# Gate and up projections of a SwiGLU feed-forward as Strassen products, with the on-chip memory laid out anew

## The chip, the cores and the metric

The kernel runs on one core of a Trainium2 chip. What is measured is the time of one execution on the device in microseconds (us), from the first to the last instruction and what lies around them. Smaller is better. The core has five engines that work beside each other and wait for each other through semaphores: TensorE (PE, matmul), VectorE (DVE), ScalarE (ACT), GpSimd (POOL) and SyncE (SP, which here only issues DMAs). Matmul results go to PSUM, eight banks of 128 x 512 floats; everything else lies in SBUF.

## The reference

Two decoder layers over 1024 tokens of width 1024 in float32. Each layer mixes tokens in three head groups, maps them by one output projection, and then runs the dense feed-forward on which the change works (D_FF = 2816):

```python
mix = jnp.concatenate([hm, ha, hs], axis=-1) @ w_out
x = x + rms_norm(mix, norm_w[1])
h = rms_norm(x, norm_w[2])
ff = (jax.nn.silu(h @ w_gate) * (h @ w_up)) @ w_down
return x + rms_norm(ff, norm_w[3])
```

`h @ w_gate` and `h @ w_up` are each 1024 x 1024 by 1024 x 2816; `@ w_down` is 1024 x 2816 by 2816 x 1024.

## The kernel before

Every engine runs one fixed instruction list, written out by hand; waits on counted semaphores (`d_hi(L, n)` is "n of layer L are done") tie the lists together. Nothing is reordered. A layer has three stages. Stage A makes the input projection, the indexer and the attention; stage B scans the chunks of the two recurrent groups and then runs the output projection and its norms; stage E is the feed-forward, and its last part is interleaved with the norm at the start of the next layer.

**Splitting.** A float32 product is made of three fp32r matmuls: each operand is split into a rounded part (`hi`, a copy on ACT) and the rest (`lo`, a subtraction), and hi\*hi + hi\*lo + lo\*hi is accumulated. A weight tile costs one ACT copy and one POOL subtraction.

**Output projection (end of stage B).** For each of the eight token tiles t (128 tokens) PE runs 48 matmuls of 128 x 512 into two PSUM banks. Then ACT takes the mean square (`stats`, count `d_s1`), DVE scales (`mixn`, `d_mix`) and adds the residual (`xres`, `d_x`), ACT takes the mean square again (`d_s2`), DVE scales (`mixn` again, `d_xn`), PE transposes the tile (`turn_normed`, 8 small matmuls, `d_turn`), ACT copies it out of PSUM as `act_hi` (`hi(t)`, `d_hi`) and DVE subtracts to get `act_lo` (`lo(t)`, `d_lo`). PE works on tile t+1 meanwhile.

**Feed-forward (stage E).** FB = 11 blocks of 256 hidden columns. A block has four units (gate and up for each of two groups of 128 columns). A unit is the product of a 1024 x 128 weight tile with all 1024 tokens: two halves of 512 tokens, 8 slices of the inner dimension, 3 matmuls each, so 48 matmuls of 128 x 512 (`half_unit`, L2125). ACT applies SiLU to the gate unit from PSUM (`gate`), DVE multiplies with the up unit from PSUM into `hf` (`hid`, L2189), ACT and POOL split `hf` into `hhi` and `hlo`. `down` then runs 96 matmuls (L2157), 12 for each token tile, and DVE adds each tile's two banks into `yacc` (L2196). PE does gate and up of block b, then down of block b-1; the last down follows on the down of the block before it. Each weight tile is a 512 KB DMA into one of two `raw` buffers, split by ACT (L2048) and POOL (L2002). At the entry PE begins with the first halves of gate and up for tokens 0 to 511 while tile 7 is still being normalised:

```python
half_unit(0, 0)
turn_normed(pe, NT - 1)
pe.wait_ge(*w_lo(L, U_FF + 2))
pe.wait_ge(*d_mix(L, NT))
half_unit(1, 0)
pe.wait_ge(*d_lo(L, NT))
half_unit(0, 1)
half_unit(1, 1)
```

**End of the layer.** Per token tile, behind its part of the last down: `yacc` add on DVE, mean square on ACT, scaling on DVE (L2219), residual add on POOL (L2041, which waits for all eight `resid` loads), and in layer 0 a mean square, a scaling (L402), a transposition on PE (L2145) and a split for layer 1.

SBUF is allotted by stacks that overlay the stages.

## Time and profile before

| | |
|---|---|
| median of 3 runs | 2903.09 us (2901.5 to 7317.59) |
| the profiled execution | 2905.06 us, of which the span is 2903.3 us |
| PE busy | 97% of the span, 13396 matmuls |
| DVE, ACT, POOL busy | 42%, 32%, 31% |
| mean granted TensorE clock | 0.984 |

The profiled execution is 2 us above the median; the sum of the prediction is made against it. A busy share counts time in which an engine has an instruction under way. Matmuls overlap in the pipeline (one takes 389 ns from start to end, yet the next starts earlier), so what a matmul costs is read from the spacing of starts.

### The profile page before, as it was taken

How to read it: one execution, taken by the hardware profiler on the slowest of the kernel's cores; microseconds unless marked ns; L12 is line 12 of the kernel's file. 1: busy time of each engine (PE TensorE's matmuls, PEld its weight loads, DVE VectorE, ACT ScalarE, POOL GpSimd, SP SyncE). 2: the span in 40 equal slices, each digit the busy share in tenths (PEclk: the TensorE clock that was granted, in tenths of full speed). 3: DMA queues.
4: the chain of work that ended last, by engine and by line, in shares of the span. 5: the costliest groups of instructions: out<-in, count | busy, mean ns of one | idle time of the engine just before them, and what ended most of it. 6: DMA issues, size and time to landing. Idle time of an engine off the chain costs nothing. (4 is left out here: it accounts for less than half of the span.)

```text
span 2903.3 us, 34251 instructions
## 1 busy us (share of the span) xinstructions
PE 2810.1 (97%) x13396; PEld 2261.9 (78%) x13396; DVE 1229.7 (42%) x2170; ACT 924.5 (32%) x1618; POOL 906.3 (31%) x450
## 2 busy tenths in 40 slices
PE   6999999999999999999989999998999999999997
PEld 5677877778888888888766788777788888888886
DVE  4479854574111122211355799547640122211115
ACT  4336433563211111111243374346632111111112
POOL 1238410330332333222343383104303232222234
PEclk9999999899999999999999999999999999999999
DMA  4102310522211111111321133106221111111113
GB/s 131 44 23 87 116 57 19 151 88 95 74 44 51 58 43 58 43 43 43 116 80 30 30 95 111 59 15 179 81 89 50 58 44 57 43 43 43 51 45 137
DMA packets 232832, 197.72 MB, mean 68 GB/s; under 512 B 20352, under 2 KB 208896, under 8 KB 232592
## 3 DMA queue, kind: packets, MB, share of 16 engines
q1 hardware_dynamic: 226960, 175.26, 20.0%
q10 hardware_dynamic: 5760, 20.97, 1.9%
q8 instruction: 70, 1.15, 0.2%
q14 instruction: 42, 0.34, 0.0%
HBM read 157.41 MB, written 38.80 MB: 68 GB/s over the span
## 5 line engine op out<-in xcount | busy, mean ns | idle before, releaser
L2125 PE MATMUL ps<-act_hi,whi 128*128 128x512 f32 x1408 | 548.4, 389 | 0.0
L2125 PE MATMUL ps<-act_hi,wlo 128*128 128x512 f32 x1408 | 548.1, 389 | 0.0
L2125 PE MATMUL ps<-act_lo,whi 128*128 128x512 f32 x1408 | 547.7, 389 | 0.0
L2189 DVE TENSOR_TENSOR hf<-sg,ps 128x1024 f32<-128x1024 f32 x44 | 53.7, 1221 | 891.4 <-PE ps L2125 891.4
L834 PE MATMUL ps<-act_hi,whi 128*128 128x512 f32 x960 | 395.2, 412 | 15.5 <-ACT smr L383 10.6
L834 PE MATMUL ps<-act_hi,wlo 128*128 128x512 f32 x960 | 378.9, 395 | 0.0
L834 PE MATMUL ps<-act_lo,whi 128*128 128x512 f32 x960 | 378.6, 394 | 0.0
L2002 POOL TENSOR_TENSOR wlo<-raw,whi 128x1024 fp32r<-128x1024 f32 x88 | 210.0, 2395 | 489.3 <-ACT whi L2048 489.3
L1247 DVE TENSOR_SCALAR_CACHE_REDUCE ties<-score,kth 128x384 uint8<-128x384 f32 (+5 forms) x396 | 348.4, 943 | 5.1 <-issue 0.4
L2196 DVE TENSOR_TENSOR yacc<-yacc,ps 128x1024 f32<-128x1024 f32 x176 | 214.8, 1220 | 248.5 <-PE ps L2157 248.5
L2125 PEld LDWEIGHTS ps<-act_lo,whi 128*128 128x128 f32 x1408 | 264.3, 188 | 55.2
L2125 PEld LDWEIGHTS ps<-act_hi,wlo 128*128 128x128 f32 x1408 | 264.3, 188 | 55.1
L2125 PEld LDWEIGHTS ps<-act_hi,whi 128*128 128x128 f32 x1408 | 264.3, 188 | 54.6
L2054 ACT ACTIVATE sg<-ps 128x1024 f32<-128x1024 f32 x44 | 45.2, 1028 | 712.8 <-PE ps L2125 712.8
L536 POOL TENSOR_TENSOR wlo<-raw,whi 128x1024 fp32r<-128x1024 f32 x56 | 137.0, 2447 | 405.4 <-ACT whi L578 405.4
L834 PEld LDWEIGHTS ps<-act_hi,whi 128*128 128x128 f32 x960 | 182.8, 190 | 90.6 <-issue 49.0
L2157 PE MATMUL ps<-dlo,hhi 128*128 128x512 f32 x640 | 249.2, 389 | 0.0
L2157 PE MATMUL ps<-dhi,hhi 128*128 128x512 f32 x640 | 249.1, 389 | 0.0
L2157 PE MATMUL ps<-dhi,hlo 128*128 128x512 f32 x640 | 249.1, 389 | 0.0
L834 PEld LDWEIGHTS ps<-act_hi,wlo 128*128 128x128 f32 x960 | 182.8, 190 | 40.0
L834 PEld LDWEIGHTS ps<-act_lo,whi 128*128 128x128 f32 x960 | 183.3, 191 | 36.1 <-issue 1.9
L2007 POOL TENSOR_TENSOR hlo<-hf,hhi 128x1024 fp32r<-128x1024 f32 x44 | 105.8, 2405 | 330.5 <-ACT hhi L2058 330.5
(304 smaller groups left out, 3974.6 us busy)
## 6 DMA issues: line engine op xcount, KB each, us to landing
raw<-in_w_in SPq DMA_DIRECT2D x56, 512.0 KB, 3.9
raw<-in_w_up SPq DMA_DIRECT2D x44, 512.0 KB, 4.0
raw<-in_w_gate SPq DMA_DIRECT2D x44, 512.0 KB, 3.8
raw<-in_w_down SPq DMA_DIRECT2D x44, 512.0 KB, 3.6
proj_scratch<-stage ACTq DMA_DIRECT2D x40, 512.0 KB, 2.7
wc<-proj_scratch SPq DMA_DIRECT2D x14, 1280.0 KB, 6.7
xmid_scratch<-xres SPq DMA_DIRECT2D x16, 512.0 KB, 2.6
resid<-xmid_scratch SPq DMA_DIRECT2D x14, 512.0 KB, 5.5
```

The source lines that it names most:

```text
L536: pool.tensor_tensor(wlo[u % 2][:, :], raw[u % 2][:, :], whi[u % 2][:, :].bitcast(F32), ALU.subtract)\
L834: mm = pe.matmul(ps[:, half, :], w[:, k], a[:, k, cols], start=(k == 0 and m == 0), stop=(k == KT - 1 and m == 2))
L1247: v.tensor_scalar(tie(c), of(c), at(kth, c), 0.0, op, ALU.add, accum_out=at(held, c))
L2002: pool.tensor_tensor(lo_t[s][:, :], raw[s][:, :], hi_t[s][:, :].bitcast(F32), ALU.subtract)\
L2007: pool.tensor_tensor(hlo[p][:, j], hf[:, :], hhi[p][:, j].bitcast(F32), ALU.subtract).then_inc(h_lo.sem, 1)
L2054: act.activation(sg[:, :], unit_psum(0), ACT.Silu).then_inc(silu.sem, 1)
L2125: mm = pe.matmul(ps[:, 2 * s + half, :], w[:, k], a[:, k, cols], start=(k == 0 and m == 0), stop=(k == KT - 1 and m == 2))
L2157: mm = pe.matmul(place(t)[:, cols], h[p][:, j, rows], w[j][:, cols], start=(j == 0 and m == 0), stop=(j == 1 and m == 2))
L2189: v.tensor_tensor(hf[:, :], sg[:, :], unit_psum(1), ALU.mult).then_inc(hidden.sem, 1)
L2196: v.tensor_tensor(yacc[:, t], yacc[:, t], place(t), ALU.add).then_inc(y_add.sem, 1)
```

## The change

**Strassen.** The gate product of a pair of units (256 hidden columns) is seen as a 2 x 2 by 2 x 2 product: the weights in four quadrants (half of the inner dimension by unit), the tokens in four (half of the inner dimension by 512 tokens). Instead of eight quadrant products, 96 matmuls, PE makes seven, of 12 matmuls each (`product`). The same is done for up. The seven token operands ("token forms": five sums of quadrants and two plain quadrants) are made once a layer and kept in SBUF, split in hi and lo. The seven weight operands ("weight forms") are made for every product: DVE adds two quadrants (five of seven), ACT copies the hi part, POOL subtracts the lo part, in a ring of six slots of 128 x 512. A slot is taken again when PE has finished with it (`f_done`).

**Results.** A product lands in one PSUM bank (banks 0 to 3 in turn; down uses 4 to 7). ACT writes the first product to two quarters of the result in SBUF, DVE adds or copies the other six into their quarters, 10 operations of 128 x 512. SiLU and the multiplication by up then run on quarters in SBUF (4 each per block instead of 2 of 128 x 1024 from PSUM).

**Order.** PE's turn k: seven products of up (k), seven of gate (k+1), then down (k), 96 matmuls as before. Gate 0 is the entry; after the tenth turn come up (10) and down (10), one behind the other. The weights come as 1 MB loads of 256 columns.

**Entry.** The token forms need float32 quadrants: ACT copies each transposed tile to `normed_q` (`untransposed`, two operations), the token sums run on DVE, their hi copies on ACT, their lo parts on DVE and POOL. They and the first weight forms are put between the steps of tiles 5, 6 and 7. The forms of tokens 0 to 511 in tiles 4 to 6 come first (`EARLIER`), tile 7 later (`LAST`). `yacc` lies where the quadrants were, so POOL clears it only when the last token form is done.

**Memory.** SBUF is placed by address. The constant table (1.3 MB) is overlaid by `yacc` and loaded again in layer 1; the small weights of layer 1 and the norm rows are loaded near the end of stage E instead of at its start. The identity for transpositions has a place of its own, so that `cst` in matmuls becomes `ident`.

The core of the diff:

```diff
+        WEIGHT_SUM = {1: ((0, 1), (1, 1), ALU.subtract), 2: ((0, 0), (1, 1), ALU.add), 3: ((1, 0), (0, 0), ALU.subtract),
+                      4: ((1, 0), (1, 1), ALU.add), 6: ((0, 0), (0, 1), ALU.add)}
+        WEIGHT_PART = {0: (1, 1), 5: (0, 0)}
+        TOKEN_SUM = {0: ((0, 0), (0, 1), ALU.add), 2: ((0, 0), (1, 1), ALU.add), 4: ((0, 1), (1, 1), ALU.subtract),
+                     5: ((1, 0), (1, 1), ALU.add), 6: ((1, 0), (0, 0), ALU.subtract)}
+        TOKEN_PART = {1: (0, 0), 3: (1, 1)}
+        SUMMED = {1: 1, 2: 2, 3: 3, 4: 4, 6: 5}
+        PRODUCT_BANK = (0, 1, 2, 3, 0, 1, 2)
...
+            def token_sum(v, i, cols):
+
+                (a, b, op), d = TOKEN_SUM[i], form_sum[i]
+                v.tensor_tensor(d[:, :, cols], normed_q[a[0]][a[1]][:, :, cols], normed_q[b[0]][b[1]][:, :, cols], op)\
+                 .then_inc(t_sum.sem, 1)
...
+            def first_form_hi(act, i):
+
+                if i in WEIGHT_SUM:
+                    act.wait_ge(*f_sum(L, SUMMED[i]))
+                    src = flat_form(ring_sum[(i + 5) % 6])
+                else:
+                    act.wait_ge(*f_in[0](L, 16))
+                    src = weight_part(ff_raw[0], *WEIGHT_PART[i])
+                act.activation(flat_form(ring_hi[(i + 5) % 6]), src, ACT.Copy).then_inc(f_hi.sem, 1)
...
-                for s in range(2):
-                    pool.wait_ge(*w_hi(L, U_FF + s + 1))
-                    if s == 1:
-                        pool.wait_ge(*wo_lo_v(L, KT - WO_POOL))
-                    pool.tensor_tensor(wlo[s][:, :], raw[s][:, :], whi[s][:, :].bitcast(F32), ALU.subtract).then_inc(w_lo.sem, 1)
+                pool.wait_ge(*t_hi(L, 1))
+                token_lo(pool, 1, EVERY, t_lo_p)
+                first_form_lo(pool, 0)
+                pool.wait_ge(*t_hi(L, 2))
+                token_lo(pool, 0, EVERY, t_lo_p)
+                for i in range(1, 4):
+                    first_form_lo(pool, i)
 
...
+                def untransposed(t):
                     act.wait_ge(*d_turn(L, t + 1))
-                    act.activation(act_hi[:, :, t * P:(t + 1) * P], tiles(turn_bank(t)), ACT.Copy).then_inc(d_hi.sem, 1)
+                    for j in range(2):
+                        ins = act.activation(normed_q[t // 4][j][:, :, (t % 4) * P:(t % 4 + 1) * P], tiles(turn_bank(t))[:, 4 * j:4 * j + 4],
+                                             ACT.Copy)
+                    ins.then_inc(d_hi.sem, 1)
...
+                    if t == NT - 1:
+                        act.wait_ge(*t_sum(L, 2))
+                        token_hi(act, 2, EARLIER)
...
+                    if t == 5:
+                        act.wait_ge(*d_hi(L, 4))
+                        token_hi(act, 1, EVERY)
+                        first_form_hi(act, 0)
+                    if t == 6:
+                        act.wait_ge(*t_sum(L, 1))
+                        token_hi(act, 0, EVERY)
+                        for i in range(1, 4):
+                            first_form_hi(act, i)
+                token_hi(act, 3, EARLIER)
+                act.wait_ge(*t_sum(L, 3))
+                token_hi(act, 4, EARLIER)
+                untransposed(NT - 1)
+                act.wait_ge(*t_sum(L, 4))
+                token_hi(act, 2, LAST)
+                act.wait_ge(*d_hi(L, NT))
+                token_hi(act, 3, LAST)
+                act.wait_ge(*t_sum(L, 5))
+                token_hi(act, 4, LAST)
+                first_form_hi(act, 4)
+                first_form_hi(act, 5)
+                for i in (5, 6):
+                    act.wait_ge(*t_sum(L, i + 1))
+                    token_hi(act, i, EVERY)
...
                 for t in range(NT):
                     s = t % 2
-                    if t == 2:
-                        lo(0)
+                    if t == NT - 1:
+                        v.wait_ge(*d_mm(L, NT))
+                        v.wait_ge(*d_hi(L, NT - 1))
+                        token_sum(v, 2, EARLIER)
...
+                    if t == NT - 1:
+                        token_sum(v, 4, EARLIER)
...
+                    if t == 6:
+                        for i in range(1, 4):
+                            first_sum(v, i)
+
+                def lo(i, cols, at_hi):
+                    v.wait_ge(*t_hi(L, at_hi))
+                    token_lo(v, i, cols, t_lo_v)
+
+                lo(2, EARLIER, 3)
+                v.wait_ge(*d_xn(L, NT))
+                first_sum(v, 4)
+                lo(4, EARLIER, 5)
+                v.wait_ge(*d_hi(L, NT))
+                token_sum(v, 2, LAST)
+                token_sum(v, 4, LAST)
+                lo(2, LAST, 6)
+                lo(3, LAST, 7)
+                lo(4, LAST, 8)
+                token_sum(v, 5, EVERY)
+                token_sum(v, 6, EVERY)
+                lo(5, EVERY, 9)
...
+                pool.wait_ge(*t_hi(L, 4))
+                token_lo(pool, 3, EARLIER, t_lo_p)
                 if N < DEPTH:
-                    clear_small(pool)
-                for i in range(2):
-                    pool.memset(yacc[:, 4 * i:4 * i + 4], 0.0).then_inc(y_add.sem, 1)
-                for b in range(3):
-                    body(b, b % 2, U_FF + max(6 * b - 2, 0))
+                    clear_columns(pool)
+                first_form_lo(pool, 4)
+                first_form_lo(pool, 5)
+                form_lo_part(6, 6, 5, (0, 1))
+                pool.wait_ge(*t_lo_v(L, 7))
+                pool.wait_ge(*t_lo_p(L, 3))
+                for t in range(NT):
+                    ins = pool.memset(yacc[t][:, :], 0.0)
+                    if t % 4 == 3:
+                        ins.then_inc(y_add.sem, 1)
...
+                k, f0 = FB - 1, cycle(FB - 1)
+                form_lo_part(6, f0 + 6, 0, (1, 0))
+                for q in range(4):
+                    down_lo(q, f0 + 7 + q, 1 + q, (0, 0))
+                    if q == 1:
+                        hid_lo(k, 0)
+                if N < DEPTH:
+                    pool.wait_ge(*f_lo(L, N_FORMS))
+                    clear_small(pool)
+                for n in range(1, 4):
+                    hid_lo(k, n)
...
+                def first_product(t, f):
+
+                    act.wait_ge(*f_done(L, f + 1))
+                    act.activation(quarter_of(t, 0, 1), ps[:, PRODUCT_BANK[0], :], ACT.Copy)
+                    act.activation(quarter_of(t, 0, 0), ps[:, PRODUCT_BANK[0], :], ACT.Copy, scale=-1.0).then_inc(m_first.sem, 1)
...
+                def product(i, f, slot, r):
+
+                    pe.wait_ge(*f_lo(L, f + 1))
+                    later = not (isinstance(r, int) and r == 0)
+                    if i == 0 and later:
+                        pe.wait_ge(*m_drain(L, 10 * (r - 1) + DRAINED[4]))
+                    if i == 1 and later:
+                        pe.wait_ge(*m_drain(L, 10 * (r - 1) + DRAINED[5]))
+                    if i == 2 and later:
+                        pe.wait_ge(*m_drain(L, 10 * (r - 1) + DRAINED[6]))
+                    if i == 4:
+                        pe.wait_ge(*m_first(L, r + 1))
+                    if i == 5:
+                        pe.wait_ge(*m_drain(L, 10 * r + DRAINED[1]))
+                    if i == 6:
+                        pe.wait_ge(*m_drain(L, 10 * r + DRAINED[2]))
+                    wh, wl = flat_form(ring_hi[slot]), flat_form(ring_lo[slot])
+                    for k in range(4):
+                        for m, (w, a) in enumerate(((wh, form_hi[i]), (wh, form_lo[i]), (wl, form_hi[i]))):
+                            mm = pe.matmul(ps[:, PRODUCT_BANK[i], :], w[:, k], a[:, k], start=(k == 0 and m == 0), stop=(k == 3 and m == 2))
+                    mm.then_inc(f_done.sem, 1)
+
...
+                def turn_of(k):
+                    f0 = cycle(k)
+                    for i in range(7):
+                        product(i, f0 + i, i % 6, up_item(k))
+                    for i in range(7):
+                        product(i, f0 + 7 + i, (i + 1) % 6, gate_item(k))
+                    down(k, f0 + 14, (2, 3, 4, 5), turn_bank)
+
...
+                product(0, 0, 5, 0)
+                product(1, 1, 0, 0)
                 turn_normed(pe, NT - 1)
-                pe.wait_ge(*w_lo(L, U_FF + 2))
                 pe.wait_ge(*d_mix(L, NT))
-                half_unit(1, 0)
-                pe.wait_ge(*d_lo(L, NT))
-                half_unit(0, 1)
-                half_unit(1, 1)
-                gate_up(0, U_FF)
...
+                def drain(t, i, f, r):
+
+                    def add(quarter, op, after):
+                        q = quarter_of(t, *quarter)
+                        v.wait_ge(*m_drain(L, 10 * r + after))
+                        v.tensor_tensor(q, q, ps[:, PRODUCT_BANK[i], :], op).then_inc(m_drain.sem, 1)
+
+                    def copy(quarter):
+                        v.tensor_copy(quarter_of(t, *quarter), ps[:, PRODUCT_BANK[i], :]).then_inc(m_drain.sem, 1)
+
+                    v.wait_ge(*f_done(L, f + 1))
+                    if i == 1:
+                        v.wait_ge(*m_first(L, r + 1))
+                        q = quarter_of(t, 0, 1)
+                        v.tensor_tensor(q, q, ps[:, PRODUCT_BANK[i], :], ALU.add).then_inc(m_drain.sem, 1)
+                        copy((1, 1))
+                    if i == 2:
+                        q = quarter_of(t, 0, 0)
+                        v.tensor_tensor(q, q, ps[:, PRODUCT_BANK[i], :], ALU.add).then_inc(m_drain.sem, 1)
```

**ScalarE, from the second mean square of tile 6 to the last tile, layer 0.** `normed10` and `normed11` are float32 quadrants, `form_hi2` the hi part of token form 2, `ring_hi0` that of a weight form in slot 0. Before:

```order
L1392 ACTIVATE mixn0,small<-xres0 128x1024 [waits d_x]
L1394 ACTIVATE small<-small 128x1 [waits d_s2]
L1396 ACTIVATE small<-small 128x1 [waits d_s2]
L1392 ACTIVATE mixn1,small<-ps 128x1024 [waits d_turn,d_mm]
L1394 ACTIVATE small<-small 128x1 [waits d_s1]
L1396 ACTIVATE small<-small 128x1 [waits d_s1]
L1787 ACTIVATE act_hi<-ps 128x8x128 [waits d_turn]
L1392 ACTIVATE mixn1,small<-xres1 128x1024 [waits d_x]
```

Now:

```order
L1458 ACTIVATE form_hi0<-form_sum0 128x2048 [waits t_sum]
L1483 ACTIVATE ring_hi0<-ring_sum0 128x512 [waits f_sum]
L1483 ACTIVATE ring_hi1<-ring_sum1 128x512 [waits f_sum]
L1483 ACTIVATE ring_hi2<-ring_sum2 128x512 [waits f_sum]
L1506 ACTIVATE mixn1,small<-ps 128x1024 [waits d_turn,d_mm]
L1508 ACTIVATE small<-small 128x1 [waits d_s1]
L1510 ACTIVATE small<-small 128x1 [waits d_s1]
L1903 ACTIVATE normed10<-ps 128x4x128 [waits d_turn]
L1903 ACTIVATE normed11<-ps 128x4x128
L1458 ACTIVATE form_hi2<-form_sum2 128x4x384 [waits t_sum]
L1506 ACTIVATE mixn1,small<-xres1 128x1024 [waits d_x]
```

Four copies stand between the last mean square of tile 6 and the first of tile 7, three of which wait for sums of DVE.

**VectorE, the same place, from the last scaling of tile 6 on.** `ring_sum` is a float32 weight sum, `form_sum` a token sum. Before:

```order
L1929 SCALAR_TENSOR_TENSOR mixn0<-xres0,small,nrow1 128x1024 [waits d_s2]
L1921 SCALAR_TENSOR_TENSOR mixn1<-ps,small,nrow0 128x1024 [waits d_s1]
L1925 TENSOR_TENSOR xres1<-xres1,mixn1 128x1024 [waits xr_in1,d_mix]
L1913 TENSOR_TENSOR act_lo<-ps,act_hi 128x8x128 [waits d_hi]
L1929 SCALAR_TENSOR_TENSOR mixn1<-xres1,small,nrow1 128x1024 [waits d_s2]
```

Now:

```order
L1472 TENSOR_TENSOR ring_sum0<-ff_raw0 128x512 [waits f_in0]
L1472 TENSOR_TENSOR ring_sum1<-ff_raw0 128x512
L1472 TENSOR_TENSOR ring_sum2<-ff_raw0 128x512
L1449 TENSOR_TENSOR form_sum2<-normed00,normed11 128x4x384 [waits d_hi,d_mm]
L2054 SCALAR_TENSOR_TENSOR mixn1<-ps,small,nrow0 128x1024 [waits d_s1]
L2058 TENSOR_TENSOR xres1<-xres1,mixn1 128x1024 [waits xr_in1,d_mix]
L1449 TENSOR_TENSOR form_sum4<-normed01,normed11 128x4x384
L2062 SCALAR_TENSOR_TENSOR mixn1<-xres1,small,nrow1 128x1024 [waits d_s2]
L1462 TENSOR_TENSOR form_lo2<-form_sum2,form_hi2 128x4x384 [waits t_hi]
L1472 TENSOR_TENSOR ring_sum3<-ff_raw0 128x512 [waits d_xn]
L1462 TENSOR_TENSOR form_lo4<-form_sum4,form_hi4 128x4x384 [waits t_hi]
```

Two token sums stand among the steps of tile 7, and two lo parts and a sum behind them.

**GpSimd at the entry of the feed-forward.** `ring_lo0` is the lo part of a weight form. Before:

```order
L357 MEMSET smw 128x1024
L358 MEMSET bcol 128x4
L2029 MEMSET yacc 128x4096 x2
L2002 TENSOR_TENSOR wlo0<-raw0,whi0 128x1024
L2007 TENSOR_TENSOR hlo0<-hf,hhi0 128x1024
```

Now:

```order
L1462 TENSOR_TENSOR form_lo3<-normed11,form_hi3 128x4x384
L415 MEMSET bcol 128x4
L1489 TENSOR_TENSOR ring_lo3<-ring_sum3,ring_hi3 128x512
L1489 TENSOR_TENSOR ring_lo4<-ff_raw0,ring_hi4 128x512
L2177 TENSOR_TENSOR ring_lo5<-ring_sum5,ring_hi5 128x512
L2219 MEMSET yacc0 128x1024
...
L2219 MEMSET yacc7 128x1024
L2177 TENSOR_TENSOR ring_lo0<-ff_raw1,ring_hi0 128x512
L2177 TENSOR_TENSOR ring_lo1<-ring_sum1,ring_hi1 128x512
```

The clearing has moved from before the first split of the stage to between the forms of gate 0 and those of up 0.

## Rows read from the trace of the kernel before

**Rows 1.** The page, busy time (share of the span) and instructions of each engine.

```profile
PE 2810.1 (97%) x13396; PEld 2261.9 (78%) x13396; DVE 1229.7 (42%) x2170; ACT 924.5 (32%) x1618; POOL 906.3 (31%) x450
```

**Rows 2.** The chain that ended last, layer 1: start us, us, what.

```profile
2173.74 81.62 PE ps L2125 x360
2255.36 21.79 PE ps L2157 x96
2277.16 43.55 PE ps L2125 x192
```

**Rows 3.** Busy time of each engine from 740 to 1400 us (feed-forward, layer 0).

```profile
740.00:1400.00 660.00, 660.00 (x2911) 546.17 (x2910) 114.79 (x94) 104.12 (x106) 199.66 (x84) 1.00 0.18 51
```

**Rows 4.** Timeline of DVE and ACT, operations of 128 x 512: start, us, engine, line.

```profile
628.63 0.68 DVE L1880 TENSOR_TENSOR smem<-smem,ps 128x512 f32<-128x512 f32 x1
628.22 0.60 ACT L1732 ACTIVATE act_hi<-ps 128x512 fp32r<-128x512 f32 x1 [1.12 <-PE ps L1565]
```

**Rows 5.** Operations of 128 x 1024 by line: ns min/median/max; and ACT's copy.

```profile
L2196 DVE TENSOR_TENSOR yacc<-yacc,ps x176: 1205/1221/1224, 823.4 to 2891.0; 128x1024 f32<-128x1024 f32 x176
L2002 POOL TENSOR_TENSOR wlo<-raw,whi x88: 2382/2396/2407, 751.9 to 2850.7; 128x1024 fp32r<-128x1024 f32 x88
750.79 1.05 ACT L2048 ACTIVATE whi<-raw 128x1024 fp32r<-128x1024 f32 x1
```

**Rows 6.** Timeline of POOL and of DVE at the start of layer 1.

```profile
1468.61 3.46 POOL L374 TENSOR_TENSOR wlo<-smw,whi 128x1024 fp32r<-128x1024 f32 x1
1472.04 3.35 POOL L2041 TENSOR_TENSOR resid<-resid,yacc 128x1024 f32<-128x1024 f32 x1
1468.59 1.27 DVE L2219 SCALAR_TENSOR_TENSOR yacc<-yacc,small,nrow 128x1024 f32<-128x1024 f32 x1
1470.33 2.83 DVE L402 SCALAR_TENSOR_TENSOR yacc<-hf,small,nrow 128x1024 f32<-128x1024 f32 x1 [0.47 <-ACT small L391]
```

**Rows 7.** Timeline of PE around tile 7, layer 0.

```profile
731.22 0.48 PE L2125 MATMUL ps<-act_hi,whi 128*128 128x512 f32 x1
...
737.81 1.09 PE L1387 MATMUL ps<-cst,mixn 128*128 128x128 f32 x8 [0.88 <-DVE mixn L1929]
738.66 0.47 PE L2125 MATMUL ps<-act_hi,whi 128*128 128x512 f32 x1
```

**Rows 8.** Timeline of ACT and DVE around tiles 6 and 7, layer 0.

```profile
722.75 1.06 ACT L1392 ACTIVATE mixn<-xres 128x1024 f32<-128x1024 f32 x1 [1.69 <-DVE xres L1925]
...
730.62 1.03 ACT L1392 ACTIVATE mixn<-ps 128x1024 f32<-128x1024 f32 x1 [6.26 <-PE ps L1635]
...
724.40 1.28 DVE L1929 SCALAR_TENSOR_TENSOR mixn<-xres,small,nrow 128x1024 f32<-128x1024 f32 x1 [0.55 <-ACT small L1396]
732.24 1.28 DVE L1921 SCALAR_TENSOR_TENSOR mixn<-ps,small,nrow 128x1024 f32<-128x1024 f32 x1 [6.56 <-ACT small L1396]
733.56 1.23 DVE L1925 TENSOR_TENSOR xres<-xres,mixn 128x1024 f32<-128x1024 f32 x1
```

**Rows 9.** Timeline of POOL at the entry of the feed-forward, layer 0.

```profile
739.89 6.98 POOL L2029 MEMSET yacc<- 128x4096 f32 x2
```

**Rows 10.** Timeline of PE at the start of layer 1: spacing of matmuls behind a wait.

```profile
1472.22 0.47 PE L834 MATMUL ps<-act_hi,whi 128*128 128x512 f32 x1 [4.04 <-POOL wlo L374]
...
1474.26 0.63 PE L834 MATMUL ps<-act_hi,whi 128*128 128x512 f32 x1
1474.68 0.63 PE L834 MATMUL ps<-act_lo,whi 128*128 128x512 f32 x1
```

**Rows 11.** Timeline of PE at the first matmul of the last down, layer 0.

```profile
1430.30 0.40 PE L2157 MATMUL ps<-whi,hhi 128*128 128x512 f32 x1
```

**Rows 12.** The tail of layer 1 on POOL, DMA around the residual loads of layer 0 (window), and DMA issues (KB, us to landing).

```profile
2873.41 2.41 POOL L2041 TENSOR_TENSOR resid<-resid,yacc 128x1024 f32<-128x1024 f32 x1 [20.36 <-DVE yacc L2219]
1410.00:1420.00 10.00, 10.00 (x46) 1.00 0.57 218
cst<-in_table SPq DMA_DIRECT2D x1, 1344.5 KB, 7.3
```

More of the change, by code:

```diff
@@ L160, in build, with at @@
         minus_b = sb("minus_b", [P, P], BF16)
-        mix_mem = ExitStack()
-        def mb(name, shape, dt=F32):
-            return sb(name, shape, dt, mix_mem)
+        def at(place, name, shape, dt=F32):
+            gap = ExitStack()
+            if place:
+                sb("to_" + name, [P, place // 4], F32, gap)
+            t = sb(name, shape, dt, gap)
+            gap.close()
+            return t
+        KB = 1024
+        act_hi = [at(32 * KB * h, f"act_hi{h}", [P, KT, HALF], F32R) for h in range(2)]
@@ L252, in build, with after @@
[L252 to L257 removed]
+        top = [MIX]
+        def after(name, shape, dt=F32):
+            t = at(top[0], name, shape, dt)
+            n = (4 if dt != U8 else 1) * int(np.prod(shape[1:]))
+            top[0] += -(-n // 32) * 32
+            return t
@@ new lines, in build @@
+        avr = after("avr", [P, NT, AH * HD])
+        aq = after("aq", [P, 2, S])
+        ak = after("ak", [P, 2, S])
+        iq = after("iq", [P, 2, S])
+        stage = [after(f"stage{s}", [P, 3 + S]) for s in range(2)]
+        ik = after("ik", [P, S])
+        smr = after("smr", [P, S])
+        ties = after("ties", [P, sum(width[2:])], U8)
+        kth = after("kth", [P, NT - 2])
+        held = after("held", [P, NT - 2])
+        TAIL = CHUNKS + 101536
+        DOWN0 = TAIL - 4 * KB
+        assert top[0] <= TAIL - 12 * KB
@@ L2139, in turn_next, with down @@
+                def down(k, f, slots, place, turning=False):
                     def turn_next(t):
```

788 lines of the change are left out of this document (462 added, 326 removed).

## The prediction

> **What bounds the kernel now.** I read the page first. PE is busy for 97% of the span, the other engines for 31 to 42% [rows 1]. A busy share alone does not name the bound, so the chain of work that ended last comes next: from 2173.74 us on it is PE alone through the whole feed-forward, in a pattern that repeats every 65.34 us, 192 gate and up matmuls in 43.55 us and 96 down matmuls in 21.79 us [rows 2]. Both give 0.227 us for a matmul of 128 x 512. The third view is the busy time by window: over 660 us of the feed-forward PE is busy without a break at a granted clock of 1.00, while DVE works 115 us, ACT 104 and POOL 200 [rows 3]. So in this stage the number of matmuls is the time, and the others have room. Around the stage, where tiles are normalised, chains through ACT, DVE and POOL decide, and PE has little slack.
>
> **Fewer matmuls.** A product pair has 7 x 12 = 84 matmuls instead of 96. A layer has 11 blocks with two such pairs, so 22 x 12 = 264 matmuls fall away, 528 in all. At 0.227 us [rows 2] that is 119.8 us, all on the path.
>
> **The work added per block (hidden).** A block becomes 168 + 96 = 264 matmuls, 59.9 us. Prices for 128 x 512: DVE 0.68 us, ACT 0.60 [rows 4]; POOL half of 2.40 = 1.20 [rows 5]. DVE: 20 result operations, 10 weight sums and 4 multiplications are 34 x 0.68 = 23, and 8 `yacc` adds of 1.22 [rows 5] make 33 us. ACT: 4 first results, 18 weight copies, 4 SiLU, 4 hidden copies, 30 x 0.60 = 18 us. POOL: 18 weight and 4 hidden subtractions, 22 x 1.20 = 26 us. All stay under 59.9.
>
> DVE and POOL also block each other. An operation of DVE with both inputs in SBUF took 2.83 us instead of 1.28 while POOL worked: it started at 1470.33 and ended at 1473.16, right after POOL's had ended at 1472.07, and POOL's next, already due, took 3.35 us instead of 2.40, so the one that waits gets the port between two instructions of the other [rows 6]. An operation with one input in PSUM never waits (1205 to 1224 ns in 176 cases beside POOL's work) [rows 5]. The weight sums and the four multiplications are of the first kind. If all 14 waited for a whole POOL operation, DVE would be held 33 + 17 = 50 us, still under 59.9. The Trainium skill, "SBUF — State Buffer", section "Who interferes with whom", states the same as a lock: a DVE instruction with two SBUF inputs and a GpSimd instruction that reads SBUF exclude each other for a whole instruction. It speaks against the change, since the sums are all of that kind; without it the entry below would come to 14.6 us a layer instead of 24.3, and the time to 2829 instead of 2849 us. The trace agrees with the rule.
>
> The tightest place of the ring is behind down (k). Two products are ready (5.44 us of PE), the third needs DVE's last `yacc` add, its sum, ACT's copy and POOL's subtraction: 1.22 + 0.68 + 0.60 + 1.20 = 3.7 us, or 5.5 with one wait for the other engine's operation at each of the two (1.20 and 0.60). It fits; I take 0. The loads: the 1.3 MB table lands in 7.3 us [rows 12]; a 1 MB weight load is let go when the forms of the previous product are made, which is at least 8 us before its first use. I take 0.
>
> **The entry to the feed-forward (twice).** Times from 730.62, when ACT begins with tile 7 in layer 0 [rows 8]. Before: PE starts the first 24 matmuls at +0.6, waits 0.88, transposes tile 7 at +7.2 and never stops from +8.0 on [rows 7]. Now, with prices scaled by length (DVE 128 x 1536 1.7, x 2048 2.25; ACT 1.5 and 1.95; POOL 3.6 and 4.8 us, from rows 4 and 5):
> - Tile 6 runs up to 0.3 late behind POOL's work; DVE ends its last scaling at -4.7 (before: 724.40 + 1.28 = -4.9) [rows 8]. The three weight sums follow, but POOL's 4.8 us subtraction for token form 0 starts at about -3.5 among them, until +1.3. The third sum ends at +2.0, ACT's copy of it at +2.6.
> - ACT's mean square of tile 7 stands behind that copy: 2.5 instead of 0. Until 4.0; then the two copies of tile 6 to 5.1. DVE's token sum 2 needs those and waits for POOL's three weight parts: 5.6 to 7.3. Then scaling 8.5, residual 9.8, mean square 11.4, scaling behind token sum 4 12.8. PE transposes tile 7 at +12.9 instead of +7.2. It has made its two products by +6.8.
> - ACT first copies forms 3 and 4 (to 14.4), then tile 7 (15.5). DVE's lo of form 2 runs to 14.4, POOL's of form 3 to 18.0, and DVE's next sum waits for it; sum, lo of form 4, two sums for tile 7 and the lo of form 2 end at 22.4. Product 2 starts at +22.4, where PE before had done as many matmuls at +8.0: **14.4 us lost**.
> - From there product 4 needs bank 0 free; ACT copies that only behind token forms 5 and 6, at +11.3. Product 5 needs DVE's two results of product 1, at +14.5, behind two sums and two lo parts of 2048 and two waits for POOL. The last lo part ends at +12.6, the lo of weight form 6 at +15.1; then POOL clears `yacc` in 7.1 us (6.98 before for the same size) [rows 9] and makes the first form of up 0: +23.5. Five products take 13.6 us: **9.9 lost**.
>
> Together 24.3 us a layer. Pauses also cost clock: after a pause of 4.04 us the spacing went to 0.43 us [rows 10] for some 7 matmuls, 1.2 GHz in place of 2.4, about 1.5 us; I take one such per entry. So 2 x 25.8 = 51.6 us. Bounds: without any mutual blocking the same queues give tile 7 transposed at +9.7, product 2 at +15.5 and up 0 20.7 after it, 7.5 + 7.1 = 14.6 lost, 2 x 14.6 = 29; at the other end 2 x 29 = 58 with one more POOL operation waited for at each half and a second spell of half clock.
>
> **The end of the feed-forward (twice).** Before, the last down follows the one before it without a gap, its first matmul 0.23 us after the last of that [rows 11], because its hidden units were made meanwhile. Now it follows up (10). Behind the last product stand: DVE result and multiplication, ACT copy, POOL subtraction, 0.68 + 0.68 + 0.60 + 1.20, and POOL still has the third quarter's subtraction in front. Worked through the queues it is 3.6 us, and 4.4 in layer 0, where the clearing of `smw` stands there too. With 1 us of half clock each: 10.0 us in all (6 to 14).
>
> **The change of layers and the rest.** The `resid` loads start only in the last block. Eight of 512 KB and two norm rows at 218 GB/s [rows 12], 2.4 us each, land about 26 us after product 2 of up (10), some 3 us after POOL could use them in layer 0; in layer 1 the tail begins 8.1 us after its last down starts, at 2873.41 [rows 12], and the loads are just in time. I take 2 us (0 to 5). The reloaded table is asked for only about 15 us later: 0. Stages A and B keep their instructions: 0.
>
> **Sum.** 2905.06 - 119.8 + 51.6 + 10.0 + 2.0 = 2848.9 us, 1.9% under the median of 2903.09. (The profiled execution is 2 us above it, which I leave in.) The bounds give 2820 to 2862. About 2% is what a measurement of this kernel can tell from no change; that line is 2845.
>
> **Rivals.**
> 1. *The entry is cheaper.* The chains above add up waits between three queues, each decided by tenths of a microsecond; with no mutual blocking they give 2829. For it: a POOL operation that comes just later finds DVE between two waits. Against: the rows show the block every time the two meet. 2829, chance 0.18.
> 2. *Something recurs in every turn.* The third form behind down has 5.44 us for 3.7 to 5.5. If it comes 1 us late, 20 turns of 1 us give 2869. For it: three engines hand over in a row. Against: all have room. Chance 0.16.
> 3. *Slower than before.* The same place, but with a pause long enough to drop the clock: 4 us and 1.5 us of half rate, as in rows 10, in each of 20 turns are 110 us, 2959. It is slower than before from 2.8 us a turn on (56 us over 20), so if that form takes over 8 us. Nothing in rows 4 to 6 reaches that. Chance 0.05.
> 4. *The saving is not taken by PE.* If what 12 matmuls save is waited for elsewhere, for PSUM banks or sums, the time would be 2905 + 64 - 120 x (share saved); with half saved 2909. Against: each bank is free 4 products before it is needed again. Chance 0.05.
>
> The forecast itself has 0.56, spread over 2835 to 2862. The range 2826 to 2873 leaves out rivals 3 and 4 and the edges of 1 and 2.
>
> **Chances.** Faster by over 2% (under 2845): rival 1 and about 0.24 of the forecast's 0.56, 0.43 with some hundredths for gains not seen. Slower by over 2% (over 2961): 0.03. Within 2%: 0.54.
>
> **What would show it.** In the feed-forward 264 matmuls of 0.227 us per block and no wait of PE longer than some tenths inside the turns. At the entry a first mean square of tile 7 that starts about 2.5 us after its matmuls, a transposition near +12.9, product 2 near +22, waits of PE for DVE's lo part, for ACT's first result and for POOL's first form behind the memsets. At the end a pause of about 4 us before the last down. I am wrong if PE waits in each turn, if DVE's adds from PSUM are slowed by POOL, or if the chains of tile 7 are much shorter than queued here.

## The result, and the profile after

The changed kernel takes 2873.56 us (median of 4 runs, 2871.85 to 2875.19) where the kernel before takes 2903.09 (median of 2901.5, 2903.09 and 2908.02; a fourth execution, of 7317.59 us, is left out as slow): a ratio of 0.9896, with a 95% interval of 0.9884 to 0.9909. The change brought some 30 us, not the 56 us that the prediction gave it, and the time lies just above the upper end of the range. Its profiled execution took 2874.07 us, with a span of 2872.2.

The page of the changed kernel, answering to [rows 1]: PE is less busy, DVE and POOL more.

```profile
PE 2737.7 (95%) x12868; PEld 2172.7 (76%) x12868; DVE 1812.2 (63%) x2886; ACT 1117.7 (39%) x2094; POOL 1233.6 (43%) x776
```

The chain of work in layer 1, answering to [rows 2] (start us, us, what):

```profile
2186.13 7.16 POOL yacc L2219 x8
2193.30 1.24 POOL ring_lo L2177
2194.54 0.04 issue
2194.59 39.37 PE ps L2394 x168
2233.95 22.21 PE ps L2419 x96
2256.16 39.12 PE ps L2394 x168
2295.29 22.21 PE ps L2419 x96
```

Read it twice. First, the pattern is what was forecast: 168 and 96 matmuls, PE alone, no pause between the pieces. Second, divide. 39.12 / 168 is 232.9 ns and 22.21 / 96 is 231.4 ns, where before 43.55 / 192 was 226.8 and 21.79 / 96 was 227.0 [rows 2]. Every matmul has the same shape as before and takes about 5.5 ns longer in the mean. A turn is 61.33 us instead of the 59.9 that 264 matmuls of 0.227 make, and from the first matmul of up 0 to the last before the pause at the end 2724 matmuls take 632.9 us instead of 617.8: 15.1 us a layer, 30.2 in all.

It is not the clock, and it is not a busy engine. Busy times from 780 to 1400 us, with the columns of [rows 3]: granted clock 1.00, DVE busy 61% of the time, POOL 53%.

```profile
780.00:1400.00 620.00, 620.00 (x2671) 500.79 (x2670) 375.34 (x427) 176.10 (x304) 330.27 (x225) 1.00 0.17 53
```

The entry of layer 0, on DVE, POOL, ACT and PE, answering to [rows 7] and [rows 8] (start us, us, engine, line):

```profile
724.10 6.30 DVE L1472 TENSOR_TENSOR ring_sum<-ff_raw 128x512 f32<-128x512 f32 x3
...
742.69 3.91 DVE L1472 TENSOR_TENSOR ring_sum<-ff_raw 128x512 f32<-128x512 f32 x1
...
724.76 5.09 POOL L1462 TENSOR_TENSOR form_lo<-form_sum,form_hi 128x2048 fp32r<-128x2048 f32 x1 [4.70 <-ACT form_hi L1458]
...
741.24 4.81 POOL L1462 TENSOR_TENSOR form_lo<-normed,form_hi 128x1536 fp32r<-128x1536 f32 x1 [7.18 <-ACT form_hi L1458]
...
765.01 7.22 POOL L2219 MEMSET yacc<- 128x1024 f32 x8
...
730.97 1.01 ACT L1506 ACTIVATE mixn<-ps 128x1024 f32<-128x1024 f32 x1
...
741.16 1.97 PE L1501 MATMUL ps<-ident,mixn 128*128 128x128 f32 x8 [5.41 <-DVE mixn L2062]
750.36 0.77 PE L2394 MATMUL ps<-form_hi,ring_hi 128*128 128x512 f32 x1 [7.23 <-issue]
...
761.11 0.48 PE L2394 MATMUL ps<-form_hi,ring_hi 128*128 128x512 f32 x1 [2.95 <-ACT gate_t L2270]
```

Three weight sums of 0.68 us took 6.30 us because POOL's subtraction of 5.09 us lay among them, and the one at 742.69 took 3.91 for the same reason. Tile 7's statistics wait for them. Count from the end of the output projection (728.67 + 0.4 = 729.07), which answers to the 730.62 of the prediction: statistics at +1.9, transposition at +12.1, product 2 at +21.3, then product 4 10.8 later and up 0 23.2 later.

The end of the feed-forward, answering to [rows 11]: PE is idle for 4.15 us before the last down, waiting for POOL. From here on a pause is counted from the start of the last matmul before it to the start of the first behind it, here 4.54 us.

```profile
1406.24 0.40 PE L2394 MATMUL ps<-form_hi,ring_lo 128*128 128x512 f32 x1
1410.79 0.76 PE L2419 MATMUL ps<-ring_hi,hhi 128*128 128x512 f32 x1 [4.15 <-POOL hlo L2188]
```

### The profile page after: what moved, and what is told of

Its sections match the earlier page's. It is cut to its first block and busy times, and to the rows that moved or that the text cites. A ratio compares the mean times of both kernels' runs of the same rounds, so it can differ in the third digit from the quotient of the medians.

```text
span 2872.2 us, 36030 instructions
## 1 busy us (share of the span) xinstructions
PE 2737.7 (95%) x12868; PEld 2172.7 (76%) x12868; DVE 1812.2 (63%) x2886; ACT 1117.7 (39%) x2094; POOL 1233.6 (43%) x776
## 5 line engine op out<-in xcount | busy, mean ns | idle before, releaser
L2177 POOL TENSOR_TENSOR ring_lo<-ring_sum,ring_hi 128x512 fp32r<-128x512 f32 x212 | 321.3, 1530 | 508.9 <-ACT ring_hi L2258 508.9
L2394 PE MATMUL ps<-form_hi,ring_hi 128*128 128x512 f32 x1232 | 491.1, 399 | 24.1 <-issue 14.5
L2394 PE MATMUL ps<-form_hi,ring_lo 128*128 128x512 f32 x1232 | 488.9, 397 | 0.0
L2394 PE MATMUL ps<-form_lo,ring_hi 128*128 128x512 f32 x1232 | 488.3, 396 | 0.0
L900 PE MATMUL ps<-act_hi,whi 128*128 128x512 f32 x960 | 396.0, 412 | 14.6 <-ACT smr L440 10.5
L900 PE MATMUL ps<-act_hi,wlo 128*128 128x512 f32 x960 | 380.0, 396 | 0.0
L900 PE MATMUL ps<-act_lo,whi 128*128 128x512 f32 x960 | 379.5, 395 | 0.0
L2419 PE MATMUL ps<-ring_hi,hhi 128*128 128x512 f32 x704 | 281.2, 399 | 8.5 <-POOL hlo L2188 8.1
L2419 PE MATMUL ps<-ring_hi,hlo 128*128 128x512 f32 x704 | 279.6, 397 | 0.0
L2419 PE MATMUL ps<-ring_lo,hhi 128*128 128x512 f32 x704 | 279.3, 397 | 0.0
L2394 PEld LDWEIGHTS ps<-form_hi,ring_lo 128*128 128x128 f32 x1232 | 232.9, 189 | 57.1
L2394 PEld LDWEIGHTS ps<-form_lo,ring_hi 128*128 128x128 f32 x1232 | 233.3, 189 | 56.0
```

Source lines behind the costliest of these rows:

```text
L900: mm = pe.matmul(ps[:, half, :], w[:, k], a[half][:, k, :], start=(k == 0 and m == 0), stop=(k == KT - 1 and m == 2))
L2177: pool.tensor_tensor(flat_form(ring_lo[slot]), src, flat_form(ring_hi[slot]).bitcast(F32), ALU.subtract)\
L2394: mm = pe.matmul(ps[:, PRODUCT_BANK[i], :], w[:, k], a[:, k], start=(k == 0 and m == 0), stop=(k == 3 and m == 2))
L2419: mm = pe.matmul(place(t)[:, cols], h[:, j, rows], w, start=(j == 0 and m == 0), stop=(j == 1 and m == 2))
```

## The experiments

**What makes a matmul 5.5 ns longer.** The trace of before holds the answer in a place that the prediction did not look at: the output projection, L1635. Its chain of work in layer 1 (start us, us, what):

```profile
2105.93 11.20 PE ps L1635 x48
```

11.20 / 48 is 233.3 ns, at full clock, for the same shape. The 96 matmuls of the last down, L2157 with whi as its moving operand, take 233.2 ns too, while the same line with dhi takes 227.0. So in the old kernel the operand tiles already decided. Where they stand in SBUF, in bytes modulo 256 by the memory plan of each program:

| matmuls | stationary | moving | spacing, ns |
|---|---|---|---|
| before, gate and up | whi, wlo 128 | act 128 | 226.8 |
| before, down | hhi, hlo 96 | dhi, dlo 96 | 227.0 |
| before, last down | hhi, hlo 96 | whi, wlo 128 | 233.2 |
| before, output projection | act 128 | wohi, wolo 32 (two of eight: 192) | 234.3 (229.7) |
| after, gate and up, by product | ring 64 or 128 | form 96, 64 or 224 | 229.7 to 234.0 |
| after, down | hhi, hlo 64 | ring 64 or 128 | 231.4 |

My theory: the spacing is short only where the operands have equal addresses modulo some number. The rival is that the instructions, the waits or the other engines' work lengthen it. Four kernels tell these apart, three made from the kernel before by one unused tile, and one from the changed kernel by moving its plan.

The gap is 64 bytes here, and `[P, 64]` (256 bytes) and `[P, 128]` (512 bytes) in the other two:

```diff
+        sb("gap", [P, 16])
         whi = [sb(f"whi{s}", [P, D], F32R) for s in range(2)]
```

> The kernel before, with nothing changed but 64 unused bytes in front of whi, so that act_hi/act_lo (moving) and whi/wlo (stationary) no longer stand at addresses that are equal modulo 512 bytes; dhi/dlo and hhi/hlo move together and stay equal. Theory (the addresses of the two operands set the spacing of the matmuls): the 4224 gate and up matmuls go from 226.9 to 231 to 234 ns, the down matmuls stay at 227.0 ns; 20 to 30 us more in the feed-forward, and up to 15 us more in the projections. Rival (the spacing of the changed kernel comes from its instructions, its waits or the work of the other engines): no change, 2905 us, spacing 226.9 ns.

Measured: 2934.11 us, ratio 1.0104 (1.0085 to 1.0123). The chain shows gate and up at 44.79 / 192 = 233.3 ns and down unchanged:

```profile
2273.48 21.77 PE ps L2158 x96
2295.26 44.79 PE ps L2126 x192
```

One tile of 64 unused bytes makes this kernel 30 us slower, with no instruction changed. The feed-forward has 27 of them: from the end of the output projection to the last down it takes 713.3 us a layer instead of 699.7.

> As the run with 64 bytes, but a gap of 256 bytes. Theory with modulus 512: gate and up matmuls slow down as well, 230 to 234 ns. Theory with a modulus of 64, 128 or 256 bytes: 226.9 ns and 2905 us as before. Rival (not the addresses): 226.9 ns, 2905 us.

Measured: 2903.62 us, ratio 0.9996 (0.9984 to 1.0007), and the spacing of before. So the modulus is 256 or a divisor of it.

```profile
2253.87 21.79 PE ps L2158 x96
2275.66 43.55 PE ps L2126 x192
```

> The control: a gap of 512 bytes, so that the operands are again equal modulo 512. Theory with modulus 512 or less: 226.9 ns, 2905 us, no change. Only a theory of a larger modulus (1024 or more) has it slower, 230 to 234 ns.

Measured: 2903.15 us, ratio 0.9989 (0.9976 to 1.0001), 226.8 ns.

```profile
2276.16 43.55 PE ps L2126 x192
```

The fourth, from the changed kernel:

```diff
-        NROW = CONST + 10784
+        NROW = CONST + 11264
...
-        CHUNKS = MIX + 8 * KB + 2496
+        CHUNKS = MIX + 8 * KB + 2560
...
-        assert top[0] == CHUNKS
+        assert top[0] <= CHUNKS
+        top[0] = CHUNKS
...
-        TAIL = CHUNKS + 101536
+        TAIL = CHUNKS + 101888
...
-        KEEP = top[0]
+        KEEP = top[0] = CHUNKS + 81408
```

> The changed kernel, with its memory plan moved by 480, 64 and 352 bytes at three places, so that every form, every ring slot, hhi, hlo and wohi/wolo stand at the same address modulo 512. No instruction changes. Theory (addresses): the feed-forward's matmuls go from 232.5 to about 227 to 229 ns, 20 to 38 us less, 2836 to 2853 us. Rival (instructions, waits or the other engines set the spacing): 2873.5 us, 232.5 ns.

Measured: 2834.0 us, ratio 0.9758 (0.9741 to 0.9775) to before, 39.6 us under the changed kernel. Its chain: 38.08 / 168 = 226.7 ns and 21.76 / 96 = 226.7 ns. DVE is busy 63% and POOL 54% of the feed-forward here (371.03 and 318.12 of 590 us), so the rival falls: the same instructions beside the same work of the other engines run at the short spacing. The spacing accounts for some 35 of the 39.6 us: 30.7 in the feed-forward from up 0 to up (10) (632.7 to 617.3 us a layer), and 3.9 in the output projection (100.5 to 98.5 us a layer), whose tiles this edit also brought to equal addresses. The rest is no more than what single runs of this kernel differ by (2830.56 to 2839.63).

```profile
2287.02 38.08 PE ps L2395 x168
2325.10 21.76 PE ps L2420 x96
```

The busy times of the same kernel from 780 to 1370 us:

```profile
780.00:1370.00 590.00, 590.00 (x2605) 488.54 (x2604) 371.03 (x412) 170.91 (x297) 318.12 (x216) 1.00 0.16 52
```

**How equal, and which operands.**

> The kernel before with 128 unused bytes in front of whi. The gap of 64 bytes brought 233.3 ns, 256 and 512 bytes 226.8 ns. If the two operands have to be equal modulo 256 bytes, the gate and up matmuls take 231 to 234 ns and the kernel some 2925 to 2935 us; if modulo 128 is enough, 226.8 ns and 2904 us.

Measured: 2937.52 us, ratio 1.0096 (1.0068 to 1.0125); the chain has 44.62 us for 192, 232.4 ns. Equal modulo 128 is not enough: of the differences tried, 0, 256 and 512 bytes are fast, 64 and 128 slow, and in the table above 32 and 96 are slow too.

```profile
2299.96 44.62 PE ps L2126 x192
```

```diff
+        sb("gap0", [P, 16])
         act_lo = sb("act_lo", [P, KT, S], F32R)
+        sb("gap1", [P, 48])
```

> The kernel before with act_lo alone moved by 64 bytes; act_hi, whi and wlo keep their places modulo 256. Two of three gate and up matmuls then still have equal operands, the third (act_lo with whi) has not, and each act_lo stands between two matmuls that stream act_hi. If what counts is the operand streamed against the weights loaded beside it, some of the three kinds slow down to 231 to 235 ns and others stay at 227: a mean of 229 to 232 ns and 2912 to 2925 us. If only the weights against the moving operand of hi and hi counted, or the stationary tile alone, there would be no change, 2904 us.

Measured: 2935.77 us, ratio 1.0101 (1.0072 to 1.0129). The chain:

```profile
2297.14 44.54 PE ps L2127 x192
```

That is 232.0 ns as a mean, and neither expectation held. All three kinds slow down alike: act_hi with whi to 231.4, act_lo with whi to 232.2, act_hi with wlo to 232.4 ns, though two of them still have equal operands. So a matmul with equal operands is slow as well when others in the stream are not equal. The changed kernel shows how far this reaches. Product 2 of up has form and ring both at 64, among products that have not, and takes 229.7 ns in the mean: its first seven matmuls take 231.9 ns and its last five 226.5. (Product 2 of gate takes its ring slot at 128, and 233.3 ns throughout.) So behind unequal operands some seven equal ones pass before the short spacing is back, in each of the 20 turns. The Trainium skill, "SBUF — State Buffer", section "Who interferes with whom", gives TensorE two read ports, one for the moving operand and one for loading weights, and calls them independent. Taken at that word, the place of one operand should not matter to the other, and the gap of 64 bytes would have cost nothing; it cost 6.5 ns a matmul, and here the measurement decides. Whether the weights of the next matmul, the operand streamed just before or both have to match was not tried.

> The kernel before with gaps of 32, 64 and 96 bytes, after which act_hi, act_lo, whi, wlo, all of wohi and wolo, dhi, dlo, hhi and hlo stand at the same address modulo 256. Theory (addresses): the 768 matmuls of the output projection go from 233.3 to 227 ns and the 192 of the last down from 233.2 to 227: 4.9 and 1.2 us less, about 2898 us; the gate and up matmuls keep 226.8 ns. Rival: no change, 2904 us. Against this kernel the change at equal placement (2834 us) is worth 64 us.

Measured: 2905.01 us, ratio 1.0001 (0.9989 to 1.0013). The spacing did what the theory said: the output projection's 48 matmuls take 10.90 us where they took 11.20, which is 227.1 ns, and the whole projection 98.5 us a layer where it took 100.6. The time did not follow: the interval leaves room for a gain of 3 us, not for the expected 6.

```profile
2107.60 10.90 PE ps L1638 x48
```

The expected 6 us are smaller than what single runs of this kernel differ by: 2892.74 to 2908.89 here, 2901.16 to 2913.25 for the kernel before on the same chip. That spread arises outside the feed-forward. In the profiled executions of the kernel before, of those with a gap of 256 and 512 bytes and of this one, everything up to the output projection of layer 0 took 618.5 to 630.0 us, and the same stages of layer 1 597.2 to 603.1. The granted clock at 160 to 640 us differs too. The first row is of the kernel before, the second of this one, whose profiled execution (2890.9 us) was its fastest; the granted clock stands third from the end.

```profile
160.00:640.00 480.00, 465.53 (x2529) 368.58 (x2528) 348.12 (x856) 240.23 (x482) 176.74 (x106) 0.96 0.26 80
```

```profile
160.00:640.00 480.00, 464.58 (x2562) 367.91 (x2562) 351.48 (x859) 242.40 (x485) 176.73 (x106) 0.98 0.26 80
```

The execution with 0.98 reached the end of the output projection of layer 0 13.6 us earlier, of which the spacing explains 2.1; in layer 1 it was 5.7 us slower than the kernel before up to the same projection. What makes these stages vary is open. It is open, too, whether the gaps cost something there, since they move other tiles of these stages as well. So the shorter spacing of the output projection is shown, and a gain in the time of this kernel is not.

**The entry and the end.** The next three start from the changed kernel with equal addresses (2834.0 us).

```diff
-                engine.tensor_tensor(form_lo[i][:, :, cols], token_form(i)[:, :, cols], form_hi[i][:, :, cols].bitcast(F32),
-                                     ALU.subtract).then_inc(done.sem, 1)
+                step = P if done is t_lo_p else cols.stop - cols.start
+                for c in range(cols.start, cols.stop, step):
+                    ins = engine.tensor_tensor(form_lo[i][:, :, c:c + step], token_form(i)[:, :, c:c + step],
+                                               form_hi[i][:, :, c:c + step].bitcast(F32), ALU.subtract)
+                ins.then_inc(done.sem, 1)
```

> The changed kernel with all addresses equal modulo 512 (2834 us) and one more edit: POOL makes its parts of the token forms' low halves (4.8 to 5.1 us each at the entry) in pieces of 128 columns, some 1.25 us each for form 0. Theory (DVE's operations with two inputs in SBUF wait for the whole of POOL's operation): the third weight sum of DVE ends 2.5 to 3.5 us earlier, tile 7's statistics start that much earlier, and of the 19.4 us of pauses of PE per entry 3 to 5 us go away; 2824 to 2830 us. Rival (DVE is late there for other reasons, such as its own queue): the pauses stay, 2834 us, or 1 us more for the added instructions.

Measured: 2834.7 us, ratio 0.9753 (0.9728 to 0.9779), no gain. Half of the theory held. From the end of the output projection DVE's third sum ended 2.8 us earlier. But POOL's four pieces took 5.95 us instead of 5.07: the first two took 1.79 and 1.74 us, the last two, when DVE's sums were done, 1.27 and 1.26; product 0 started 1.3 us later and DVE's residual add took 2.27 us instead of 1.23. Up 0 started 0.6 us earlier in each layer. The first row is of the kernel with equal addresses, the second of this one:

```profile
715.43 5.07 POOL L1463 TENSOR_TENSOR form_lo<-form_sum,form_hi 128x2048 fp32r<-128x2048 f32 x1 [4.62 <-ACT form_hi L1459]
```

```profile
720.21 5.95 POOL L1465 TENSOR_TENSOR form_lo<-form_sum,form_hi 128x512 fp32r<-128x512 f32 x4 [4.63 <-ACT form_hi L1459]
```

The exclusion works in both directions, an exclusive lock, as the Trainium skill has it in the section of "SBUF — State Buffer" that the prediction names; finer pieces share the loss out anew.

The four orders, on DVE, ACT, POOL and PE:

```diff
                 lo(2, EARLIER, 3)
-                v.wait_ge(*d_xn(L, NT))
-                first_sum(v, 4)
-                lo(4, EARLIER, 5)
                 v.wait_ge(*d_hi(L, NT))
                 token_sum(v, 2, LAST)
                 token_sum(v, 4, LAST)
                 lo(2, LAST, 6)
+                first_sum(v, 4)
                 lo(3, LAST, 7)
+                lo(4, EARLIER, 5)
                 lo(4, LAST, 8)
...
+                act.wait_ge(*x_out[0](L, 16 * NT // 2))
+                act.wait_ge(*f_done(L, 1))
+                act.activation(gate_t[:, 1, 0:HALF], ps[:, 0, :], ACT.Copy)
+                act.activation(gate_t[:, 0, 0:HALF], ps[:, 0, :], ACT.Copy, scale=-1.0).then_inc(sig("m_first", 2 * FB).sem, 1)
                 for i in (5, 6):
                     act.wait_ge(*t_sum(L, i + 1))
...
-                act.wait_ge(*x_out[0](L, 16 * NT // 2))
-                first_product(gate_t, 0)
...
-                for t in range(NT):
-                    ins = pool.memset(yacc[t][:, :], 0.0)
-                    if t % 4 == 3:
-                        ins.then_inc(y_add.sem, 1)
                 for j in range(6):
                     form_lo_part(j, 7 + j, j, (1, 1))
+                    for t in ((), (0,), (1, 2), (3, 4), (5, 6), (7,))[j]:
+                        ins = pool.memset(yacc[t][:, :], 0.0)
+                        if t % 4 == 3:
+                            ins.then_inc(y_add.sem, 1)
...
-                    pe.wait_ge(*h_lo(L, 4 * k + 4))
+                    pe.wait_ge(*h_lo(L, 4 * k + (2 if isinstance(k, int) and k == FB - 1 else 4)))
                     for t in range(NT):
+                        if isinstance(k, int) and k == FB - 1 and t == NT // 2:
+                            pe.wait_ge(*h_lo(L, 4 * k + 4))
...
-                    pe.wait_ge(*t_lo_v(L, i + 1))
+                    pe.wait_ge(*t_lo_v(L, (2, 3, 5, 6, 7)[i - 2]))
```

> As a_split, and four orders changed: at the entry DVE makes the last quarter of form 2 before the weight sum 4 and form 4; ACT takes the first result of the first gate product before token forms 5 and 6; the clearing of yacc (7 us of POOL) is spread between the forms of up 0; and the last down starts when the first two quarters of its hidden units are there and waits for the other two at its fifth tile. Theory (the pauses are these queues): pause before product 2 down by 2 more us, before product 4 (3.1 us) gone, before up 0 (2.8) gone or moved to product 5, before the last down (4.8) gone, all twice: 2804 to 2818 us. Rival (each pause only moves to the next thing that is late): 2824 to 2830 us as a_split.

Measured: 2823.02 us, ratio 0.971 (0.9685 to 0.9734), between what the theory and the rival gave. Against the kernel with equal addresses, PE's pauses in layer 0 went as follows: before product 2 from 7.65 to 5.33 us, before product 4 (3.12) and before up 0 (2.77) gone, a new one of 5.70 before product 5. From the end of the output projection up 0 starts 2.9 us earlier: of 8.2 us of pauses that went, 5.7 came back at product 5. The pause before the last down went from 4.76 to 1.00 us, and in layer 1 from 4.81 to none. The spells of half clock behind them went with them (matmuls 0.43 us apart), and the last down became 2.2 and 2.3 us shorter.

The last edit, against the changed kernel as the others; POOL's subtractions are whole again:

```diff
                 lo(4, LAST, 8)
-                token_sum(v, 5, EVERY)
-                token_sum(v, 6, EVERY)
-                lo(5, EVERY, 9)
-                lo(6, EVERY, 10)
...
+                token_sum(v, 5, EVERY)
+                token_sum(v, 6, EVERY)
                 form_sum_part(6, 6, 5, (0, 1))
                 drain(gate_t, 1, 1, 0)
+                v.wait_ge(*t_hi(L, 9))
+                token_lo(v, 5, EVERY, t_lo_v)
                 drain(gate_t, 2, 2, 0)
+                v.wait_ge(*t_hi(L, 10))
+                token_lo(v, 6, EVERY, t_lo_v)
```

> a_best (2823 us) without the split of POOL's subtractions, which only delayed product 0 by 1.2 us, and with one more order: DVE takes the results of product 1 before the low halves of forms 5 and 6, which product 5 waited 5.7 us for. Theory (the queue of DVE sets product 5): that pause goes to 2 to 4 us, product 0 starts at once: 2 to 5 us less per entry, 2814 to 2820 us. Rival (the sum of DVE's and POOL's work behind tile 7 sets the end of the entry, whatever the order): 2820 to 2826 us.

Measured: 2816.57 us, ratio 0.9699 (0.9675 to 0.9724), the lowest time of all. The interval overlaps with that of the kernel before this one (0.9685 to 0.9734), which ran on another chip; the trace shows a gain of 1.3 us per entry, as up 0 starts that much earlier. The last matmul of up (10) and the first of the last down, in layer 0, against the pause of 4.54 us shown above:

```profile
1383.44 0.39 PE L2395 MATMUL ps<-form_hi,ring_lo 128*128 128x512 f32 x1
1384.43 0.47 PE L2422 MATMUL ps<-ring_hi,hhi 128*128 128x512 f32 x1 [0.60 <-POOL hlo L2191]
```

The pause at product 5 is 3.81 us (4.22 in layer 1), and up 0 starts 4.2 us earlier than with equal addresses alone (4.3 in layer 1).

```profile
759.02 0.50 PE L2395 MATMUL ps<-form_hi,ring_hi 128*128 128x512 f32 x1 [3.42 <-DVE form_lo L1465]
```

What is left at the entry is mostly DVE: in layer 1 its low halves and sums of the token forms stand in the chain from 2138.95 to 2148.49 without a gap.

```profile
2138.95 4.04 DVE form_lo L1465 x3
2142.99 5.50 DVE form_sum L1450 x2
```

## Why the prediction was wrong

**Fewer matmuls, and their price: the step that failed.** "Both give 0.227 us for a matmul of 128 x 512" was read from the two loops of before and carried over to the changed kernel, whose tiles stand elsewhere. The number of matmuls was right; the price became 0.2323. The saving of 528 was 119.8 us as predicted, and the 5448 matmuls of the turns gave back 30.2 us of it. The diff said that memory is laid out anew by address, and I gave that no price at all. The trace had one: the same shape at 233 ns in L1635. I read the durations of the two groups that the change touches, found them equal, and took the figure for a property of the shape.

**The entry, 51.6 us predicted.** From the end of the output projection up 0's place is reached at +21.8 before (752.4 with 730.62) and at +44.4 after: 22.6 us lost in layer 0 and 22.7 in layer 1, 45.3 in all, 1 us of which is the spacing. The chain went as worked out (+1.9, +12.1, +21.3 against +2.5, +12.9, +22.4), each step a little shorter, and PE waited for what was named: tile 7, the last low half of form 2, ACT's first result, POOL's form behind the memsets. Only the pause before product 5 did not come. The mechanism was right and the total 6.3 us too large, but that total hides two errors of opposite sign. The waits are some 6 us shorter per entry than the 24.3 worked out. The half clock costs more than the one spell of 1.5 us: there are two spells, behind the pauses before products 2 and 4, in which 6 to 13 matmuls start 0.43 us apart, together 3.7 us in layer 0 and 4.4 in layer 1 against a spacing of 0.232. That they offset each other in part is luck. (The lower bound of 29 for both entries leaves the half clock out.)

**The end, 10.0 us predicted.** The pauses are 4.54 us in layer 0 and 4.36 in layer 1 (4.4 and 3.6 predicted). The half clock behind them cost more than 1 us each: 13 and 11 matmuls start 0.43 us apart, and the last down took 38.7 us instead of 36.6 in layer 0 and 2.4 us more in layer 1. Together 13.4.

**The change of layers, 2.0 predicted.** Between the last down and the next projection lie 5.7 us instead of 5.3, and the tail of layer 1 is as long as before: 0.4. (Its first residual add stood 8.3 us behind the start of the last down, 2873.41 with 2865.10, not 8.1.)

**The work added per block, 0 predicted.** Right: no pause inside the turns. DVE is busy 37 us a turn and POOL 33 (33 and 26 predicted, without the waits for each other). Rivals 2, 3 and 4 did not occur: the time is near the 2869 us of rival 2, but in the turns no matmul starts more than 0.241 us behind the one before, so that is chance. Rival 1, a cheaper entry, holds for 6 of its 20 us.

**The sum again.** 2848.9 + 30.2 - 6.3 + 3.4 - 1.6 = 2874.6; the profiled execution took 2874.07. With equal addresses the kernel takes 2834.0, about 15 under the prediction. The same sum without the 30.2, and with 4 us off for the output projection, which also became faster, gives 2840.4 for it; the 6 us that remain are no larger than what single runs differ by, and no run explains them.

## What to carry to other kernels

Before taking a time per instruction over to a new version, look for the same shape elsewhere in the trace: if two places differ at full clock, something other than the shape sets the price, and it can change with an edit that is only about memory. On a kernel bound by TensorE, lay out moving and stationary tiles at equal addresses modulo 256 bytes, all tiles that follow each other in the stream alike; here it was worth 1.4% and costs under 1 KB of padding per partition. This is shown for fp32r matmuls of 128 x 512 in which every matmul loads its own weights, and for nothing else. Where three engines hand over in turn, a wait removed at one place mostly comes back at the next; the pause to go for is the one whose consumer doesn't need all that it waits for, as the last down here, which needed half of its hidden units to start.

## What was not expected of the hardware

- Matmuls of 128 x 512 in fp32r followed each other at 226.7 to 227.1 ns when all operands of the stream were equal modulo 256 bytes, and at 229.7 to 234.3 ns (means of a group) otherwise, at a granted clock of 1.00; a shift of 64 or 128 bytes cost some 30 us in 2904, one of 256 or 512 nothing.
- The penalty belongs to the stream: matmuls with equal operands slowed from 226.8 to 231.4 and 232.4 ns when only the moving tile of every third matmul was shifted by 64 bytes, and in the changed kernel seven matmuls with equal operands (231.9 ns) passed before the spacing was 226.5.
- DVE and POOL exclude each other both ways: POOL's 5.07 us became 5.95 when it was cut in four and DVE could get in between.
